# Seven block products in place of eight in the dilated stage of a fused decoder step, with weight sums on GpSimd

## The reference, cut to what matters

```python
h = rms_norm(x); z = h @ w_in                       # w_in: 1024 x (q_a, kv_a, gate_a, qkv_b, uv_c, gate_m)
q, k, v = qkv_b.reshape(b, t, 3, 3, 8, 64)          # branch B: 3 dilations x 8 heads
o_g, lse_g = banded_attention(split_residues(q_g, dil), split_residues(k_g, dil), split_residues(v_g, dil), window // dil)
o_b = combine_by_denominator(outs, lses)
new_dil_g[b] = concat([cache_dil_g[b], new rows])[-window:]
m = sigmoid(gate_m[0]) * (o_a @ wa) + sigmoid(gate_m[1]) * (o_b @ wb) + sigmoid(gate_m[2]) * (o_c @ wc)
x = x + m @ wo;  x = x + relu(rms_norm(x) @ w_up)**2 @ w_down
```

## Time and profile before

| | us |
|---|---|
| Median of 3 runs | 1829.16 (1821.88 to 1833.83) |
| The profiled execution's own time | 1845.35 |
| Its span, first to last instruction | 1843.7 |
| TensorE busy (share of the span) | 1733.6 (94%) |
| VectorE, ScalarE, GpSimd busy | 672.6, 327.6, 184.3 |
| Mean granted TensorE clock | 0.959 of full speed |

### The profile page before, as it was taken

How to read it: one execution, slowest core, us unless ns; L and a number is a source line. 1 busy time by engine, 2 the same in 40 slices (tenths; PEclk the granted TensorE clock), 3 DMA queues, 4 the chain that set the end, 5 groups by cost and what they waited for, 6 DMA issues and landing times. The chain is left out here.

```text
span 1843.7 us, 27027 instructions
## 1 busy us (share of the span) xinstructions
PE 1733.6 (94%) x10424; PEld 1376.6 (75%) x10424; DVE 672.6 (36%) x1583; ACT 327.6 (18%) x836; POOL 184.3 (10%) x329
## 2 busy tenths in 40 slices
PE   8996899999989999999996898888998999999997
PEld 3785799999968777777773455656887888888885
DVE  3432244443321333333222202102466766543234
ACT  2210034433320222222220121210000000000000
POOL 0000100000000001000006575540000000000000
PEclk9998699999989999999996989988999999999999
DMA  9999433333339987421309999895521222222221
GB/s 315 348 353 306 133 103 104 101 100 108 115 132 330 338 306 271 138 94 47 99 33 322 314 343 322 293 328 196 178 79 48 92 69 92 84 77 91 69 92 49
DMA packets 150339, 323.10 MB, mean 175 GB/s; under 512 B 18690, under 2 KB 87619, under 8 KB 149187
## 3 DMA queue, kind: packets, MB, share of 16 engines
q1 hardware_dynamic: 118498, 178.87, 29.7%
q0 software_dynamic: 27104, 129.65, 20.3%
q10 hardware_dynamic: 4608, 12.85, 2.1%
HBM read 303.89 MB, written 109.25 MB: 224 GB/s over the span
## 5 line engine op out<-in xcount | busy, mean ns | idle before, releaser
L1435 PE MATMUL bank<-hT,wring 128*128 128x272 f32 x1408 | 346.7, 397 | 1.1 <-PEq L1216 1.1
L1435 PEld LDWEIGHTS bank<-hT,wring 128*128 128x128 f32 x1408 | 260.4, 191 | 58.5 <-issue 10.5
L956 PE MATMUL bank<-wring,w 128*128 128x128 f32 x2048 | 247.3, 278 | 1.1 <-DVE hidp L871 1.1
L956 PEld LDWEIGHTS bank<-wring,w 128*128 128x128 f32 x2048 | 237.0, 193 | 10.0 <-issue 9.5
L1868 POOL DMA_DIRECT2D ring<-in_sel_pages x256 | 140.9, 551 | 321.3 <-issue 277.7
L2253 PEld LDWEIGHTS bank<-hT,xk 128*128 128x128 f32 x512 | 104.5, 210 | 54.3 <-issue 30.4
L2253 PE MATMUL bank<-hT,xk 128*128 128x272 f32 x512 | 140.4, 432 | 0.0
L2506 PE MATMUL bank<-hT,wring 128*128 128x272 f32 x392 | 95.4, 392 | 0.0
L2506 PEld LDWEIGHTS bank<-hT,wring 128*128 128x128 f32 x392 | 74.5, 190 | 15.4
L2506 PE MATMUL bank<-aT,wring 128*128 128x272 f32 x352 | 85.9, 392 | 0.0
L319 POOL DMA_DIRECT2D out_new_dil<-in_cache_dil x24 | 15.1, 635 | 675.1 <-POOLq L1216 343.5
(11 more groups left out here) (365 smaller groups left out, 2293.8 us busy)
## 6 DMA issues: line engine op xcount, KB each, us to landing
wring<-in_w SPq DMA_DIRECT2D x147, 512.0 KB, 4.4
out_new_dil<-in_cache_dil POOLq DMA_DIRECT2D x8, 8176.0 KB, 33.6
wring<-in_cmp_pages SPq DMA_DIRECT2D x256, 128.0 KB, 2.2
ring<-in_sel_pages POOLq DMA_DIRECT2D x256, 64.0 KB, 4.5
ring<-in_sel_pages SPq DMA_DIRECT2D x256, 64.0 KB, 4.1
out_new_dil<-in_cache_dil POOLq DMA_DIRECT2D x8, 2032.0 KB, 12.8
ring<-in_dil_k SPq DMA_DIRECT2D x9, 1024.0 KB, 8.3
ring<-in_dil_k POOLq DMA_DIRECT2D x9, 1024.0 KB, 7.4
```

Source lines behind the costliest of these rows:

```text
L956: last = pe.matmul(banks[6 + c % 2][:, P * part:P * part + P].rearrange("p (g a s) -> p g a s", g=G, s=8), w1[:, kv, 8 * hf + jj, :], x[:, ...
L1435: mm = pe.matmul(banks[6 + hf][:, 0:HT], ring_slot(wr, u)[:, k * P:k * P + P], hT[:, k, HT * hf:HT * hf + HT], start=(k == 0), stop=(k == ...
```

## The change

For a pair of weight units the 1024 x 256 weights are cut into four quarters (rows 0 to 511 and 512 to 1023, unit a and unit b), the activations `hT` into four (rows, columns 0 to 271 and 272 to 543). Instead of eight block products of four matmuls each, seven are made (`products_pe`), of sums and differences:

- `HH`: T1, T2, T4 in a new tile `ht` and T3 in place in `hT`, made by four VectorE subtractions of 128 x 1088 in the sparse block (after pairs n = 1, 3, 5, 7); the last one is undone by a fifth at the end of the dilated block.
- `weights_pool`: four GpSimd operations of 128 x 512 for each of the 22 pairs, two of them in place in the ring. `sum1` and `sum2` have one buffer each, so the first waits for product 5 of the pair before. Between the pairs GpSimd starts the cache copies, one for every second pair up to pair 7, then two, then three a pair; each copy waits for the copy two before it (two semaphores in place of one).
- `sums_dve`: seven VectorE additions of 128 x 272 a pair put the products together; `keeps_act`: ScalarE keeps product 1 of each pair, and applies tanh to whole gate tiles in SBUF. `half_act`, `half_dve`, `dqS`, `gst3` go.
- The products use banks 6 and 7 in turn, each bank for one product of four matmuls. In all 616 matmuls instead of 704: 140 ahead of step 0, 35 a step in steps 0 to 11, 14 a step in steps 12 to 15.
- Weights are loaded by pairs, three pairs ahead; the ring is the same. The gates 0 to 3 ride as tenth units of the head pairs.
- `max3_dve`, `exp3_act`, `norm3_dve` take one head a call, with sums between. `dv3` has one buffer where `dv2` had two.
- The input block sends four cache copies instead of five; the dilated block 28 instead of 27.

The diff, cut to its core:

```diff
--- before
+++ after
...
+GP = 8
...
-            unit(U_DIL + 9 * p + n, w_in, 1304 + n * 512 + P * p + np.arange(P))
+            unit(U_DIL + 10 * p + n, w_in, 1304 + n * 512 + P * p + np.arange(P))
...
-                if sent["n"] and sent["n"] % 2 == 0:
-                    eng.wait_ge(sm["bulk_done"], 16 * sent["n"])
+                done = sm["bulk_done" if sent["n"] % 2 == 0 else "bulk_done_odd"]
+                if sent["n"] >= 2:
+                    eng.wait_ge(done, 16 * (sent["n"] // 2))
...
+        HH = {"B11": hT[:, 0:4, 0:HT], "T3": hT[:, 0:4, HT:NT], "B21": hT[:, 4:8, 0:HT],
+              "B22": hT[:, 4:8, HT:NT]}
+        for i, name in enumerate(("T1", "T2", "T4")):
+            HH[name] = ht[:, i, :].rearrange("p (k q) -> p k q", k=4)
...
-                bulk_copies(pool, 5)
+                bulk_copies(pool, 4)
...
+                    elif n < 8:
+                        out, x, y = (("T1", "T3", "B11"), ("T2", "B22", "T1"), ("T3", "B22", "T3"),
+                                     ("T4", "B21", "T2"))[n // 2]
+                        ch.link(dve.tensor_tensor(HH[out], HH[x], HH[y], ALU.subtract))
...
+        DPAIRS = 20 + (GP - 4) // 2
+        DORDER = (1, 2, 6, 7, 4, 5, 3)
+        DREAD = {2: 1, 6: 2, 7: 3, 4: 4, 5: 6, 3: 7}
...
-                self.left = 36 if b < 12 else 16 * GP // 4
+                self.left = 35 if b < 12 else 28 * (DPAIRS - 20) // 4
...
+        def products_pe(pe, mults):
+            for m in mults:
+                p, n, k = m // 28, DORDER[m // 4 % 7], m % 4
+                q = m // 4
                 if k == 0:
+                    if n == 1:
+                        for u in range(2):
+                            unit_landed(pe, U_DIL + 2 * p + u)
+                    if n in (6, 7, 5, 3):
+                        pe.wait_ge(s_pw, 4 * p + {6: 3, 7: 2, 5: 1, 3: 4}[n])
+                    if q >= 2:
+                        pb, nb = (q - 2) // 7, DORDER[(q - 2) % 7]
+                        if nb == 1:
+                            pe.wait_ge(s_px, pb + 1)
+                        else:
+                            pe.wait_ge(s_ps, 7 * pb + DREAD[nb])
+                a11, a12, a21, a22 = quarters(p)
+                w, x = {1: (a11, "B11"), 2: (a12, "B21"), 3: (a12, "B22"), 4: (a22, "T4"),
+                        5: (sum1, "T1"), 6: (sum2, "T2"), 7: (a21, "T3")}[n]
+                mm = pe.matmul(product_bank(p, n), w[:, P * k:P * k + P], HH[x][:, k, :],
+                               start=(k == 0), stop=(k == 3))
+                if k == 3:
                     mm.then_inc(s_hf, 1)
...
+        def weights_pool(pool, p):
+            a11, a12, a21, a22 = quarters(p)
+            for u in range(2):
+                unit_landed(pool, U_DIL + 2 * p + u)
+            if p:
+                pool.wait_ge(s_hf, product_at(p - 1, 5) + 1)
+            pool.tensor_tensor(sum1, a21, a22, ALU.add).then_inc(s_pw, 1)
+            pool.wait_ge(s_pw, 4 * p + 1)
+            pool.tensor_tensor(a21, a11, a21, ALU.subtract).then_inc(s_pw, 1)
+            pool.tensor_tensor(sum2, sum1, a11, ALU.subtract).then_inc(s_pw, 1)
+            pool.wait_ge(s_pw, 4 * p + 3)
+            pool.wait_ge(s_hf, product_at(p, 2) + 1)
+            pool.tensor_tensor(a12, a12, sum2, ALU.subtract).then_inc(s_pw, 1)
...
+        def keeps_act(act, mults):
+            for p, n in ends(mults):
+                if n == 1:
+                    act.wait_ge(s_hf, product_at(p, 1) + 1)
+                    if p:
+                        act.wait_ge(s_ps, 7 * (p - 1) + 2)
+                    act.activation(px, product_bank(p, 1), ACT.Copy).then_inc(s_px, 1)
+                if n == 3:
+                    for u in range(2):
+                        s = 2 * p + u
+                        if is_gate(s):
+                            act.wait_ge(s_ps, 7 * p + 7)
+                            act.activation(unit_home(s), unit_home(s), ACT.Tanh, scale=0.5
+                                           ).then_inc(s_gt, 1)
...
+        def sums_dve(dve, mults):
+            for p, n in ends(mults):
+                if n == 1:
                     continue
+                a, b = unit_home(2 * p), unit_home(2 * p + 1)
+                at, x = 7 * p, product_bank(p, n)
+                dve.wait_ge(s_hf, product_at(p, n) + 1)
+                if n == 2:
+                    s = 2 * p
+                    if s % 10 == 0 and 20 <= s < 40:
+                        dve.wait_ge(s_st[s // 10 % 2], 16 * (s // 20))
+                    elif s >= 40:
+                        dve.wait_ge(s_st[0], 32)
+                    dve.wait_ge(s_px, p + 1)
+                    dve.tensor_tensor(a[:, 0:HT], x, px, ALU.add).then_inc(s_ps, 1)
+                elif n == 6:
+                    dve.tensor_tensor(u2, x, px, ALU.add).then_inc(s_ps, 1)
+                elif n == 7:
+                    dve.wait_ge(s_ps, at + 2)
+                    dve.tensor_tensor(u3, x, u2, ALU.add).then_inc(s_ps, 1)
+                elif n == 4:
+                    s = 2 * p + 1
+                    if s < 40 and s % 10 == 9 and s > 10:
+                        g = gate_of(s) - 1
+                        dve.wait_ge(s_gs[g % 2], 32 + 16 * (g // 2))
+                    dve.wait_ge(s_ps, at + 3)
+                    dve.tensor_tensor(b[:, 0:HT], x, u3, ALU.add).then_inc(s_ps, 1)
+                elif n == 5:
+                    dve.tensor_tensor(b[:, HT:NT], x, u3, ALU.add).then_inc(s_ps, 1)
+                    dve.tensor_tensor(u2, x, u2, ALU.add).then_inc(s_ps, 1)
+                else:
+                    dve.wait_ge(s_ps, at + 6)
+                    dve.tensor_tensor(a[:, HT:NT], x, u2, ALU.add).then_inc(s_ps, 1)
...
+            if b == 12:
+                act.wait_ge(s_gs[1], 48)
...
+                for p in range(3, DPAIRS):
+                    sp.wait_ge(s_hf, 7 * (p - 3) + 7)
+                    for u in range(2):
+                        u = U_DIL + 2 * p + u
                         sp.dma_start(ring_slot(wr, u), t["w"][u]).then_inc(w_landed[u % RING], 16)
+                    if p % 5 == 3 and p > 3:
+                        store_turn((p - 8) // 5)
+                    if p % 5 == 4 and p > 4:
+                        store_new((p - 9) // 5)
+                store_turn(3)
+                store_new(3)
+                for g in range(4, GP):
+                    store_gate(g)
...
-                bulk_copies(pool, len(bulk) - sent["n"])
+                for p in range(DPAIRS):
+                    weights_pool(pool, p)
+                    k = (1 - p % 2 if p < 8 else 2 if p < 12 else 3)
+                    bulk_copies(pool, min(k, len(bulk) - sent["n"]))
...
+                sums_dve(dve, fill.take(92))
+                mask3_dve(dve, ch, 0, (1, 2))
+                sums_dve(dve, fill.take(12))
+                mask3_dve(dve, ch, 0, (0,))
+                for hh in range(2):
+                    max3_dve(dve, ch, 0, hh)
+                    sums_dve(dve, fill.take(8))
+                for hh in range(2):
+                    norm3_dve(dve, ch, 0, hh)
+                    sums_dve(dve, fill.take(4))
+                sums_dve(dve, fill.take())
...
+                dve.wait_ge(s_hf, 7 * DPAIRS)
+                ch.count(dve.tensor_tensor(HH["T3"], HH["B22"], HH["T3"], ALU.subtract))
...
+                products_pe(pe, fill.take(92))
+                scores_ab_pe(pe, 0)
+                products_pe(pe, fill.take(12))
+                scores_c_pe(pe, 0)
+                products_pe(pe, fill.take())
```

More of the change, by code:

```diff
@@ L176, in weight_stream @@
         for h in range(2):
-            unit(U_MIX + 2 * f + h, w_in, at + f % 3 * D + two[h])
+            u = 2 * f + h
+            unit(U_MIX + u if u >= 4 else U_DIL + 10 * u + 9, w_in, at + f % 3 * D + two[h])
         w[U_BR + f] = np.concatenate([cols(br[f % 3], c) for c in two], 1).reshape(P, UNIT)
@@ L1440, in half_act @@
[L1440 to L1445, removed]
-                    continue
[L1447 to L1456, removed]
-                    act.wait_ge(s_gs[g % 2], 16 + 16 * (g // 2))
-                act.wait_ge(s_hf, h + 1)
-                act.activation(gst3[:, g % 2, HT * hf:HT * hf + HT], banks[6 + hf][:, 0:HT], ACT.Tanh,
-                               scale=0.5).then_inc(s_ev[hf], 1)
@@ L1462, in half_dve @@
-        def half_dve(dve, products):
-            for n in products:
-                h = n // 8
-                u, hf = h // 2, h % 2
-                if n % 8 < 7 or hf == 0 or u >= 36:
-                    continue
-                t = u // 9
-                if u % 9 == 0 and t >= 2:
-                    dve.wait_ge(s_st[t % 2], 16 * (t // 2))
-                dve.wait_ge(s_hf, h + 1)
-                dve.tensor_copy(dq2[:, t % 2, u % 9, HT:SEQ], banks[7][:, 0:SEQ - HT])
-                dve.tensor_copy(dqS[:, u % 9, :], banks[7][:, SEQ - HT:HT]).then_inc(s_ev[1], 1)
@@ L1475, in projected, with ends, product_at, product_bank @@
-        def projected(eng, units):
```

(36 more changed lines are left out.)

237 lines of the change are left out of this document (104 added, 133 removed).

## The result

The changed kernel takes 1783.45 us (median of 4 runs, 1777.08 to 1789.5) beside 1831.49 for the kernel before (median of 4 runs now): a ratio of 0.9719, 95% interval 0.9681 to 0.9757, or -51.4 us (-58 to -45). Forecast were -52.0 us and a median of 1777. The same kernel, timed twice more, gave 0.9673 (0.959 to 0.9757) and 0.968 (0.9638 to 0.9722), that is -60 and -59 us.

The account below looks back on a forecast made before the run. TensorE, busy 94% of the span, was taken to bound the kernel. Products -40.3, fifth copy -16.7 and late readers +5 sum to -52.0 us, from 1829.16 to a median of 1777 us, range 1762 to 1802.

Parts of the forecast that it names:

- Products: Dilated block: 88 fewer matmuls at 0.458 us each take 40.3 us off TensorE's path.
- Fifth copy: End of input block: without GpSimd's fifth copy the next block starts at 173.1 instead of 189.83, gaining 16.7 us.
- Late readers: Dilated block: VectorE reads some product banks late, 0.3 us a step, +5 us.
- The bound of 0.7 us a place: Dilated block, wide steps: up to 0.7 us late, three places a step, 16 steps: between 0 and 34 us.
- Rival B: Dilated block: VectorE reads the two short banks late, costing 20 us instead of 5; 1792 us, chance 0.12.
- GpSimd: Dilated block: the weight-sum chain stays hidden behind 5.5 us of TensorE work if one operation is below 1.73 us; cost 0.
- Rival C: Dilated block: GpSimd's sums at 3.48 us bound it, 74 us lost, 1851 us; slower than before from 3.14 us; chance 0.05.
- SBUF sharing: Dilated block: 32 normalisations could each wait for a GpSimd sum, and a sum for one; estimated +3 us, inside the late-reader range.
- Last steps, loads, GpSimd's queue, ScalarE: Dilated block: thinner cover in steps 12 to 15, pair loads, copy waits and ScalarE's store wait each cost 0.
- The clock behind the gap: After the input block: the clock still falls to half behind the short gap; 0 taken, bound 7 us of gain.
- Rival D: After the input block: the clock holds through the short gap; 1770 us, chance 0.12.
- The total: Whole kernel: -52.0 us, to a median of 1777 us and a profiled execution of 1793.4 us.

Follow-up runs that it names:

- experiment 1: The kernel before with four cache copies in the input block instead of five, nothing else of the change: ratio 0.9933 to the kernel before.
- experiment 3: The changed kernel with one more cache copy in the input block, issued from ScalarE's queue at its end: ratio 0.9741 to the kernel before.
- experiment 2: The changed kernel with five cache copies in the input block instead of four: ratio 0.9709 to the kernel before.
- experiment 5: The changed kernel with the weight sums on VectorE, GpSimd only starting copies: ratio 0.9679 to the kernel before.
- experiment 6: The changed kernel with maxima and normalisations of both heads back to back, no additions between: ratio 0.9682 to the kernel before.
- experiments 4 and 10: The changed kernel with the first weight sum made five times (4) or three times (10) in a row: ratios 1.0123 and 0.9775 to the kernel before.

## Why the prediction was right, point by point

- *Products*, -40.3 us forecast: the dilated block is 41.6 us shorter, in every kernel with 22 pairs and an unstretched chain between 382.5 and 383.9 us. 41.6 / 88 is 0.473 us; the 0.458 per matmul held to about 3%.
- *Fifth copy*, -16.7 forecast: -16.9 by the start of the block. The reading that the block's end waits for GpSimd's own DMAs is shown by experiments 1 and 3, and by the landing in experiment 2. Incomplete was "the new waits let copy 3 go when copy 1 lands, which is not later". It is earlier: 63.81 against 93 us. With five copies that alone brings 10.2 of the 16.9 us (experiment 2), as the dropped copy alone brings 16.2 (experiment 1). The number came out right for either order, since both end at the last engine's work.
- *Late readers*, +5 forecast: mis-sized, it measured 0. TensorE has no wait for an addition, nor with 60 us more work on VectorE (experiment 5), and one of 0.4 us with longer stretches between its reads (experiment 6). The bound of 0.7 us a place took the worst end of a product at every step. Rival B falls with it.
- *GpSimd*: I took an operation below 1.73 us; it is 1.27 to 1.29. The estimate from the Trainium skill (GPSIMD Engine Reference, Elementwise, side-by-side cycle accounting) was 1.35 us, and the traces agree within 6%. Rival C's mechanism exists and its threshold is right (experiments 4 and 10), but its price was too low: its sum held only the idle time, and the measured loss with stalls up to 3.9 us was 1.57 times the idle time, because the clock falls too.
- *SBUF sharing*: The Trainium skill (SBUF: two separate sides, of the page SBUF, State Buffer) says that a VectorE instruction with two SBUF inputs or in its two-port mode and one of GpSimd exclude each other for the whole instruction. The traces agree: the widest normalisation takes 0.89 us where no sum runs and 1.85 where it begins beside one, as if it stood for most of the sum. It costs the kernel nothing that can be measured, since VectorE is not waited for.
- *Last steps, loads, GpSimd's queue, ScalarE*: no new wait of TensorE in the block. The fifth subtraction of 128 x 1088 took 1.28 us, as worked out from the two shapes.

```profile
L1836 DVE TENSOR_TENSOR hT<-hT 128x1088 f32<-128x1088 f32 x1 | 1.3, 1281 | 0.0
```

- *The clock behind the gap*, 0 forecast: in the profiles of the change that is what happened. Rival D is real in other executions and is worth 9 us of the sparse block rather than 7.
- *The total* agrees better than its parts, and that is partly luck. The +5 us did not come, so the parts that did add up to -57, near the -59.2 of the two profiles and the -60 and -59 of the two later timings; that the first timing's -51.4 lies so close to -52.0 is luck within its interval (-58 to -45). The +0.3 us behind the dilated block is luck too, since that part alone differs by up to 15 us between profiles of the same code. The forecast median of 1777 was 6 us off.

## What to carry to other kernels

At the end of a block look at which engine's transfers are still under way: a copy that nobody needs can hold every engine if GpSimd issued it, here for 17 us. Price a new chain by its stalls only while they stay short; a stall of nearly 4 us also cost a slower clock behind it, one of 1.3 us did not. And where TensorE must stand for some us before a stretch of small matmuls, a few unused matmuls in the gap are worth trying.

## What the runs showed of the hardware that was not expected

- The end of a block waits for the landings of GpSimd's DMAs but not for one issued by ScalarE (experiments 1 to 3; 173.3 us with 21 us of that copy still to come, against a block that begins 0.6 us behind GpSimd's landing in two kernels).
- A stand of TensorE of 3.92 us was followed by matmuls at half speed (3.99 us for 2.00), one of 1.28 us by matmuls at full speed (2.10 and 2.00). At 3.05 us both outcomes occur from one profile to the next.
- A VectorE normalisation of 0.89 us that begins beside a GpSimd sum of 1.29 us takes 1.85 us, in three of three calls of that width that met one (experiment 5).
